# Order of tiles, weight halves, modulation pieces and filter rows in a two-layer hybrid backbone on one core

## What is computed

```
for l in range(2):
    mod = silu(c) @ w_mod[l] + b_mod[l]                    # 6 x 1024, for latents and for context
    h = modulate(rms_norm(x), mod[0], mod[1])
    p = h @ w_in[l]                                        # q, k, v, pool, hyena (v, x1, x2), 3 gates
    y0 = neighbourhood_attention(q, k, v)                  # latents also read context
    y1 = multiscale_pool(p[pool])
    z  = depthwise_conv3(p[hyena])
    for o in range(2):                                     # long convolution, filter built on the chip:
        z = gate_o * (irfft(rfft(z) * H_o) + skip * z)     # H = spectrum of sin(sin(z @ w1) @ w2) @ w3 * decay
    merged = sum_n sigmoid(p[gate n]) * (y_n @ w_branch[n])
    x = x + mod[2] * (merged @ w_out[l])
    x = x + mod[5] * top2_of_16_experts(modulate(rms_norm(x), mod[3], mod[4]))
return rms_norm(x)
```

## Time and profile before

| | |
|---|---|
| median of 3 runs | 1649.73 us (1644.4 to 1655.82) |
| the profiled execution, device time | 1645.23 us |
| its span, first to last instruction | 1643.5 us |
| PE matmul busy | 1469.4 us (89%) |
| DVE / ACT / POOL busy | 874.4 / 632.8 / 361.1 us |
| mean granted clock of PE | 0.957 of 2.4 GHz |
| chain that ended last, largest shares | PE 22%, DMA 9% (operands_plain<-in_w_up_e 6%), DVE 5% |
| matmuls under `mm3` with w_lo or w_hi and h | L946 to L948, 274.3 + 264.1 + 263.9 us and 141.1 + 137.4 + 137.5 us |

### The profile page before, as it was taken

One profiled execution on the slowest core, in us unless ns is written; L12 is line 12 of the kernel. 1 busy time (PEld: TensorE's weight loads), 2 busy tenths in 40 slices (PEclk: granted clock), 3 DMA queues, 4 the chain that ended last, 5 costly groups with the idle time before them and its releaser, 6 DMA issues. The chain is left out here.

```text
span 1643.5 us, 19883 instructions
## 1 busy us (share of the span) xinstructions
PE 1469.4 (89%) x7944; PEld 1069.4 (65%) x7944; DVE 874.4 (53%) x1252; ACT 632.8 (39%) x847; POOL 361.1 (22%) x196
## 2 busy tenths in 40 slices
PE   6998899977999997889999987898978997998887
PEld 2565679755677764678888874597867995333334
DVE  4711567685132335699999974655494565211112
ACT  2422222265122224367877763442255443010102
POOL 0322333310232231010101003183322662000000
PEclk9999999998999998999999998899999998999998
DMA  9447222201655570689999994052213677899994
GB/s 332 165 181 275 91 77 78 78 20 48 210 180 196 188 253 35 243 330 408 410 402 407 403 318 141 26 180 77 91 58 129 215 238 272 329 419 419 422 422 173
DMA packets 118029, 367.27 MB, mean 223 GB/s; under 512 B 8046, under 2 KB 73776, under 8 KB 86960
## 3 DMA queue, kind: packets, MB, share of 16 engines
q1 hardware_dynamic: 109168, 334.58, 54.2%
q0 software_dynamic: 8768, 31.40, 5.2%
HBM read 353.37 MB, written 12.58 MB: 223 GB/s over the span
## 5 line engine op out<-in xcount | busy, mean ns | idle before, releaser
L799 POOL TENSOR_TENSOR w_lo<-ring,w_hi 128x1024 fp32r<-128x1024 f32 x120 | 296.3, 2478 | 630.5 <-ACT w_hi L1748 630.5
L946 PE MATMUL bank<-h_hi,w_hi 128*128 128x512 f32 (+1 forms) x768 | 274.3, 357 | 15.2 <-DVE h_lo L2110 7.4
L947 PE MATMUL bank<-h_hi,w_lo 128*128 128x512 f32 (+1 forms) x768 | 264.1, 344 | 0.0
L948 PE MATMUL bank<-h_lo,w_hi 128*128 128x512 f32 (+1 forms) x768 | 263.9, 344 | 0.0
L946 PEld LDWEIGHTS bank<-h_hi,w_hi 128*128 128x128 f32 x768 | 147.4, 192 | 54.3 <-issue 26.0
L948 PEld LDWEIGHTS bank<-h_lo,w_hi 128*128 128x128 f32 x768 | 147.7, 192 | 17.0
L947 PEld LDWEIGHTS bank<-h_hi,w_lo 128*128 128x128 f32 x768 | 147.8, 192 | 16.4 <-issue 1.4
L946 PE MATMUL bank<-w_hi,h_hi 128*128 128x512 f32 (+1 forms) x384 | 141.1, 368 | 13.1 <-DVE w_lo L2450 5.1
L1748 ACT ACTIVATE w_hi<-ring 128x1024 fp32r<-128x1024 f32 x120 | 125.5, 1053 | 52.0 <-DMA ring<-in_w_in 28.4
L948 PE MATMUL bank<-w_lo,h_hi 128*128 128x512 f32 (+1 forms) x384 | 137.5, 358 | 0.0
L947 PE MATMUL bank<-w_hi,h_lo 128*128 128x512 f32 (+1 forms) x384 | 137.4, 358 | 0.0
(11 more groups left out here) (341 smaller groups left out, 2799.2 us busy)
## 6 DMA issues: line engine op xcount, KB each, us to landing
ring<-in_w_in SPq DMA_DIRECT2D x52, 1024.0 KB, 5.2
ring<-in_w_down_e SPq DMA_DIRECT2D x36, 1024.0 KB, 11.9
ring<-in_w_up_e SPq DMA_DIRECT2D x34, 1024.0 KB, 7.9
mix<-in_w_gate_e SPq DMA_DIRECT2D x32, 1024.0 KB, 7.9
operands_plain<-in_w_gate_e SPq DMA_DIRECT2D x29, 1024.0 KB, 22.3
ring<-in_w_mod SPq DMA_DIRECT2D x24, 1024.0 KB, 6.9
mix<-in_w_mod SPq DMA_DIRECT2D x24, 1024.0 KB, 4.9
mix<-in_w_up_e SPq DMA_DIRECT2D x22, 1024.0 KB, 23.5
```

The lines of the kernel that those rows point to most:

```text
L799: pool.tensor_tensor(w_lo[:, slot], rview(raw, 8)[:, :, x * P:(x + 1) * P], w_hi[:, slot].bitcast(F32), ALU.subtract).then_inc(w_l, 1)
L946: first = mm(dst, stat[0], mov[0], start=start, stop=False)
L947: mm(dst, stat[1], mov[0], start=False, stop=False)
L948: return first, mm(dst, stat[0], mov[1], start=False, stop=stop)
```

## The change

1. In `take_tiles` half 18 is led before the first tiles are taken, and the half led at tile g (16 to 23) is g + 3 instead of g + 2; at tile 24 half 27 follows, at tile 28 the halves 28 and 29 as before.
2. In the first branch of each merge, the gate tiles that were not made ahead (6 and 7 in layer 0, 3 in layer 1; `BEHIND` = 8, 4) are run first, before branch tile 0; ACT and DVE take their products where they did. The releases move along: `w_u` at the second of them and at branch tile 0, `ring_used` for the first half of branch weights at branch tile 4 (layer 0) or gate tile 4 (layer 1), for the second half of layer 0 at the end of the branch.
3. Layer 1's modulation pieces: 3 in branch 0 (in front of branch tile 0, behind the tiles 3 and 7), 8 in each of the others, 5 in the output projection; SP's list of issues, `mod_rows`, `mod_columns` and `mod_take` shift by one.
4. The filters' second hidden layer is computed twice, on 128 rows (w2, its bias and frequency doubled on the host), w3 is laid out with one direction on rows 0 to 63 and the other on 64 to 127, and `filters` alternates between the two row halves.

```diff
+BEHIND = [8, 4]
-        w3s = by_layer("w3s", 2048, HY_H)
+        w3s = by_layer("w3s", 1024, 2 * HY_H)
...
-            mod_behind = {base + 5: [0], base + 6: [1, 2, 3], base + 8: [4], base + 9: [5, 6, 7], base + 11: [8],
...
+            mod_behind = {base + 5: [0, 1], base + 6: [2], base + 8: [3], base + 9: [4, 5, 6],
+                          base + 11: [7], base + 12: [8, 9, 10], base + 14: [11], base + 15: [12, 13, 14],
+                          base + 17: [15], base + 18: [16, 17, 18], base + 19: [19], base + 20: [20],
+                          base + 21: [21, 22, 23]}
...
-                    mm(bank[3][0:HY_H, 0:SEQ], fw2[l], fhid[l][1], start=True, stop=True).then_inc(f_p[l], 1)
+                    mm(bank[3][:, 0:SEQ], fw2[l], fhid[l][1], start=True, stop=True).then_inc(f_p[l], 1)
...
-                for i in range(2):
-                    for j in range(2):
-                        last = mm(fbank[o][2 * i + j][:], fhid[l][2][:, j * P:(j + 1) * P],
-                                  w3s[l][:, (2 * o + i) * BW:(2 * o + i + 1) * BW], start=True, stop=True)
+                for j in range(2):
+                    for i in range(2):
+                        rows = slice(i * HY_H, (i + 1) * HY_H)
+                        last = mm(fbank[o][2 * i + j][:], fhid[l][2][rows, j * P:(j + 1) * P],
+                                  w3s[l][rows, o * BW:(o + 1) * BW], start=True, stop=True)
...
                         pe.wait_ge(g_d[l], n * DK + (m + 1))
-                        if n == 0 and m < PRE[l]:
-                            if m == 4:
-                                gate(0, PRE[l], j_pe[l], ring_used)
+                        if n == 0 and m == 0:
+                            for x in range(PRE[l], BEHIND[l]):
+                                gate(0, x, j_pe[l], w_u if x > PRE[l] else None)
+                            if l == 0:
                                 next_mod(1)
-                            branch(0, m, 2, w_u if m == 4 else None)
-                        elif n == 0 and l == 0:
-                            branch(0, m, 2)
-                            if m == DK - 1:
-                                next_mod(1)
-                                gate(0, m, j_pe[l], ring_used)
+                        if n == 0 and m < BEHIND[l]:
+                            branch(0, m, 2, w_u if m == 0 else ring_used if m == 4 else None)
                         elif m % 4 < 3:
-                            gate(n, m, g_pe[l], w_u if m == 4 else None)
+                            gate(n, m, g_pe[l], None if m != 4 else w_u if n or l == 0 else ring_used)
                             branch(n, m, 1, w_u)
                         else:
                             branch(n, m, 1)
                             gate(n, m, g_pe[l], ring_used)
-                        if l == 0 and (n or m in (3, 5)):
+                        if l == 0 and (n or m % 4 == 3):
                             next_mod(1)
-                        if l == 0 and n and m == 5:
+                        if l == 0 and n and m == 6:
                             mod_columns(1, n - 1)
-                    if n == 0 and l == 0:
-                        pe.wait_ge(j_pe[l], 32 + DK)
-                    else:
-                        pe.wait_ge(g_pe[l], n * (2 * DK) + (2 * DK))
-                    pe.nop().then_inc(w_u, 1)
+                    pe.wait_ge(g_pe[l], n * (2 * DK) + (2 * DK))
+                    pe.nop().then_inc(ring_used if n == 0 and l == 0 else w_u, 1)
...
-                    if l == 0 and m < 4:
+                    if l == 0 and m < 5:
                         next_mod(1)
-                    if l == 0 and m == 5:
+                    if l == 0 and m == 6:
                         mod_columns(1, 2)
...
-                            lead_in(g + AHEAD)
-                        elif g in (24, 28):
+                            lead_in(g + AHEAD + 1)
+                        elif g == 24:
+                            lead_in(27)
+                        elif g == 28:
                             for x in range(2):
-                                lead_in(26 + (g - 24) // 2 + x)
-                        if g >= 32:
+                                lead_in(28 + x)
+                        elif g >= 32:
                             lead_in(g - 4 + AHEAD)
...
+                lead_in(16 + AHEAD)
                 take_tiles(at_start)
...
-                    if l == 0 and m == 6:
+                    if l == 0 and m == 7:
                         mod_take(1, 2)
```

More of the change, by code:

```diff
@@ L229, in build @@
         places = [dict(w3s=0, decay=2048, fz=3072, fw1=3328, fw2=3392, fhid=4096, fang=4864, fpm=6144, fraw=8192),
-                  dict(w3s=4096, decay=6144, fz=14336, fw1=14592, fw2=14656, fang=14720, fhid=15232, fpm=12288,
+                  dict(w3s=4096, decay=6144, fz=14336, fw1=14592, fw2=15744, fang=14720, fhid=15232, fpm=12288,
                        fraw=18432, late_fpm=8192, late_fraw=0, late_fhid=22016)]
@@ L234, in by_layer @@
             return [area(p[name], n)[0:rows] for p in places]
-        w3s = by_layer("w3s", 2048, HY_H)
+        w3s = by_layer("w3s", 1024, 2 * HY_H)
         decay = [v.rearrange("p (j c) -> p j c", j=2) for v in by_layer("decay", 1024)]
[L238 to L242, removed]
+        fz, fw1, fw2 = by_layer("fz", 256, HY_E), by_layer("fw1", 64, HY_E), by_layer("fw2", 2 * HY_H, HY_H)
+        fhid = [[area(p["fhid"], 256), area(p["fhid"] + 256, 256)[0:HY_H],
+                 area(p.get("late_fhid", p["fhid"] + 512), 256)] for p in places]
+        fang = [v.rearrange("p (i t) -> p i t", i=2) for v in by_layer("fang", 512)]
         fpm, fraw = ([[area(p[n] if o == 0 else p.get("late_" + n, p[n]), 2048)
@@ L1707, in filter_sin @@
                 act.wait_ge(f_d[l], 10 * l + 1 + i)
-                A(fhid[l][1 + i], fhid[l][0], ACT.Sin).then_inc(f_a[l], 1)
+                A(fhid[l][1 + i], fhid[l][0][0:(1 + i) * HY_H], ACT.Sin).then_inc(f_a[l], 1)
             def spectrum_a(l, o):
@@ L1904, in _ @@
                             lead(q0 + 2 * IN_C + q, q % WS, q % 2, at % RS, full_at(at))
-                        if n == 0 and l == 0:
+                        if n == 0 and m < BEHIND[l]:
                             if m >= PRE[l]:
                                 act.wait_ge(j_pe[l], 32 + m + 1)
-                        elif n or m >= PRE[l]:
+                        else:
                             act.wait_ge(g_pe[l], 2 * DK * n + 2 * m + (2 if m % 4 == 3 else 1))
@@ L1921, in _ @@
                             parts_in(n + 1)
-                        if l == 0 and n and m == 4:
+                        if l == 0 and n and m == 5:
                             mod_rows(1, n - 1)
@@ L2141, in angle @@
             def angle(l, i):
-                fc = [par[l][0:HY_H, C_FILT + x:C_FILT + x + 1] for x in range(3)]
+                rows = (1 + i) * HY_H
+                fc = [par[l][0:rows, C_FILT + x:C_FILT + x + 1] for x in range(3)]
                 dve.wait_ge(f_p[l], 8 * l + i + 1)
-                x0, x1, x2 = fhid[l][0], fang[l][:, 0, :], fang[l][:, 1, :]
+                x0, x1, x2 = fhid[l][0][0:rows], fang[l][0:rows, 0, :], fang[l][0:rows, 1, :]
                 if i:
                     dve.wait_ge(f_a[l], 6 * l + 1)
-                link(V.tensor_scalar(x1, bank[2 + i][0:HY_H, 0:SEQ], fc[2 * i], fc[1], ALU.add, ALU.mult))
+                link(V.tensor_scalar(x1, bank[2 + i][0:rows, 0:SEQ], fc[2 * i], fc[1], ALU.add, ALU.mult))
                 link(V.tensor_scalar(x2, x1, 1.0 / TWO_PI, 12582912.0, ALU.mult, ALU.add))
@@ L2410, in _ @@
                             parts_in(n + 1)
-                        if l == 0 and n and m == 6:
+                        if l == 0 and n and m == 7:
                             mod_take(1, n - 1)
@@ L2843 @@
     for l in range(DEPTH):
-        filt = np.zeros((P, 3), np.float32)
-        filt[0:HY_H, 0] = hy_b1[l]
-        filt[0:HY_H, 1] = hy_freq[l]
-        filt[0:HY_H, 2] = hy_b2[l]
+        filt = np.tile(np.stack([hy_b1[l], hy_freq[l], hy_b2[l]], axis=1), (2, 1))
         data[f"par{l}"] = np.concatenate(
@@ L2859 @@
     data["router_bias"] = np.broadcast_to(np.asarray(router_bias), (P, E_N))
-    for name, v in (("w_mod", w_mod), ("w_in", w_in), ("pool_w", pool_w), ("hy_w1", hy_w1), ("hy_w2", hy_w2),
-                    ("hy_w3", hy_w3), ("w_branch", w_branch), ("w_out", w_out), ("w_gate_e", w_gate_e),
+    data["hy_w2"] = np.tile(hy_w2, (1, 1, 2))
+    data["hy_w3"] = np.asarray(hy_w3).reshape(DEPTH, HY_H, HY_O, 2, BW).transpose(0, 3, 1, 2, 4).reshape(
+        DEPTH, 2 * HY_H, HY_O * BW)
+    for name, v in (("w_mod", w_mod), ("w_in", w_in), ("pool_w", pool_w), ("hy_w1", hy_w1), ("w_branch", w_branch), ("w_out", w_out), ("w_gate_e", w_gate_e),
                     ("w_up_e", w_up_e), ("w_down_e", w_down_e)):
```

2 lines of the change are left out of this document (removed).

## The result

The changed kernel took 1636.76 us (median of 4 runs, 1634.3 to 1638.64) beside 1651.21 us of the kernel before on the same chip: a ratio of 0.9928, 95% interval 0.9908 to 0.9948. That is under 1% faster and inside the range that was predicted. The prediction's sum was 13.3 us; the two profiled executions differ by 10.9 us, the medians by 14.5. The total came out, in part by luck: its make-up did not, and most of this document is about that.

What follows compares the result with a forecast made beforehand. TensorE was taken as the bound, its matmuls filling 1469.4 of 1643.5 us. Terms 8.4 + 1.5 + 1.9 - 0.2 + 1.7 = 13.3 us gave 1632 or 1636, taken as 1634; range 1620 to 1645.

Steps and rivals of the forecast that it cites:

- Halves three ahead: Hyena stage: leading weight halves one tile earlier ends 9.55 us of PE waits for w_lo; 8.4 us gained, bounds 3 and 12.5.
- the contention that was named: Hyena stage: POOL's earlier subtractions hold DVE; 1.7 us off in layer 1's pooling chain, 0.4 us in layer 0.
- The clock gain of 1.4 us: Hyena stage: low clock after each removed wait goes in part, 0.5 us per wait, plus 1.4 us.
- the second rival: POOL, working earlier, holds DVE each round and PE waits for DVE: 3 instead of 8.4, total 8, 1639 to 1642; chance 0.14.
- Merge of layer 0: Two gate tiles moved to the front remove 9.27 us of waits, new waits return 7.75; 1.5 us gained, bounds -3 and 13.5.
- First new wait: Layer 0's merge, fifth branch tile: PE waits 3.4 us for the second weight half, as wb_hi is one buffer.
- Second: Layer 0's merge, next branch's first tile: PE waits 4.35 us because the branch weights' ring slot is given back late.
- the clock, counted even: Layer 0's merge: low-clock loss taken as equal before and after, with two gaps again.
- Merge of layer 1: One gate tile in front fills 2.88 us of a 5.73 us wait, 1.0 returns; 1.9 us gained, bounds 0 and 4.5.
- the modulation's 0.2: Output projection: the last piece's mod_take moves onto DVE's path, 0.18 us; term -0.2.
- Filters: Filters' last layer: row halves run side by side, a call takes about 1.9 us; first call gains 1.7, bounds 0 and 3.5.
- Gains go through undiminished: Whole kernel: late expert-weight loads are released by layer 1 events, so earlier gains reach the end and add one to one.

## Why the prediction was right in sum and wrong in its terms

- **Halves three ahead (8.4 predicted, 7.0 of it without clock; 3.9 measured at equal clock).** The mechanism was right: all three waits for w_lo went, and the contention that was named came. The step that failed is its size. For layer 0 the prediction took 0.4 us off, against a slack of 1.34 us in the first round, with the second round at nothing. POOL costs DVE's products 3.1 and 3.8 us in the two rounds, against 1.5 and 1.6 before, and PE waited 0.71 and 1.39 us. In the pooling chain 1.7 us were predicted and 2.1 came; further 1.26 us of wait moved to ACT's copy. The clock gain of 1.4 us was not to be seen in this part alone. By mechanism and size this is close to the second rival (3 us); the first term of the sum should have been near that one.
- **Merge of layer 0 (1.5 predicted, 2.3 in the two traces, the deferred piece taken off).** First new wait 3.4 predicted, 3.56 measured. Second 4.35 predicted, 2.96 measured: the sum left out the modulation piece that stands between the branch's end and the next gate tile (1.07 us), and SP issued 0.2 us after that piece began (422.17), not 0.5; 4.35 less 1.07 less 0.3 is 2.98. Idle time fell by 6.99 + 2.28 less 3.56 less 2.96 = 2.75 us; the clock, counted even, may have taken the rest.
- **Merge of layer 1 (1.9 predicted).** 3.57 us at the opening, and 1.5 of it back, but at the output projection behind the last branch's context weights and not at branch tile 4, where after shows no wait (0.7 us in the merges alone). Both merges alone: 2.5 us at equal clock, 3.2 predicted with the modulation's 0.2.
- **Filters (1.7 predicted, 2.3 measured, 3.4 in the traces at the start).** The call was sized right (1.9; it took 1.99). The step that failed is that the loads were not priced: going from 64 to 128 rows doubled their rate, and that freed a piece ahead of the call.
- **Gains go through undiminished.** True for the parts as a whole within the errors (8.7 against 8.2), not from stage to stage: some 3 us of lead go between 690 and 729 us, where the clock is lower than before.
- **The clock** brings 3.8 us of the gain in the means. The sum held 1.4 us of clock, in the halves' term. The rest made up for part of what the halves fell short: at equal clock the whole is 8.2 us, which is the second rival's 8 and not the forecast's 13.3 (11.9 without its clock), so that the time hit the forecast is in part luck. None of the three parts alone had the whole's clock (0.9521 to 0.9562). Why the whole has it is open: in the traces the granted clock rises from 0.96 to 1.00 over the merge of layer 1, but also over the last 33 us (0.80 to 0.85), which nothing of the change touches.

## What to carry to other kernels

When a producer off the path is told to work earlier, look up what shares its time with the engine that PE waits for next: a DVE product with both inputs in SBUF lost 0.6 to 2.3 us to one subtraction on POOL, so hold back the pieces that aren't needed yet. Work that covers a wait should stand at the place where the buffer changes hands, and a second cover at a place that one fills is taken from another. Compare variants that differ by less than 1% at equal clock and by the same instruction in two traces; a median alone hid the halves' gain and laid the clock's share of the whole to the parts. Before starts are compared, make sure that the same work stands ahead of both: here a deferred piece looked like 1.07 us of gain.

## What the runs showed of the hardware

- A load of 512 KB to 64 rows ran at 199 GB/s, to 128 rows at 416, with the DMA engines as busy in both (0.95 and 1.03). The length of a row (8 KB and 4 KB) is not the cause: the 1 MB pieces ahead of it, 8 KB to each of 128 rows, move at 426 (before, 13 to 17 us). The Trainium skill, DMA: Bandwidth & Descriptors, section The descriptor swizzle, puts rows 0 to 63 on the even ports of SBUF and rows 64 to 127 on the odd ones. The trace agrees in size: with half of the rows, half the rate. That the ports are the cause no run here shows.
- PE took products on rows 64 to 127 ahead of products on rows 0 to 63 that stand earlier in the program: 1.99 us for the call in either order.
- Beside a POOL subtraction of 2.4 us a DVE product of 0.69 us took 2.96, and a pair of edge products of 0.37 us took 2.46, where both inputs lay in SBUF; a product with one input in PSUM was not held (0.69). In all seven cases in layer 0's two rounds, before and after, the held product ended 0.54 or 0.55 us after the subtraction did.
